# Norms, gates and rotary computed between the pieces of their projections, and a compressed attention branch placed last

## The reference, cut to what matters

```python
# block 1: sparse attention with three branches, gated and summed
o = gb[..., 0:1] * o_cmp + gb[..., 1:2] * o_sel + gb[..., 2:3] * o_win

# block 2: forgetting attention (16 heads of 64)
q, k, v, fz = jnp.split(h @ w_in, [hd, 2 * hd, 3 * hd], axis=-1)
q = rms_norm(q.reshape(B, S, H, 64), q_g)        # k the same way with k_g
log_f = jax.nn.log_sigmoid(fz + fgate_b)
c = jnp.cumsum(log_f, axis=1)                    # added to the logits: c[query] - c[key]

# block 3: one projection, then attention beside a spatial gating
q, k, v, gu, gv = jnp.split(y @ w_in, 5 parts of 512)
q, k = rope(q), rope(k)
gmlp_out = gelu(gu) * (tril(w_s) @ layernorm(gelu(gv)) + b_s)
merged = concat([rmsnorm(attn_out, g_attn), rmsnorm(gmlp_out, g_gmlp)])
```

## Time and profile before

| | |
|---|---|
| median of three runs | 4069.65 us (4064.81 to 4070.16) |
| the profiled execution | 4067.28 us, span on the core 4065.5 us |
| PE / PEld busy | 92% / 84% of the span |
| DVE / ACT / POOL busy | 73% / 45% / 9% |
| granted TensorE clock, mean | 0.953 of full speed |
| DMA | 748.70 MB, mean 184 GB/s |

### The profile page before, as it was taken

How to read it: one execution, slowest core, us unless ns; L and a number is a source line. 1 busy time by engine, 2 the same in 40 slices (tenths; PEclk the granted TensorE clock), 3 DMA queues, 4 the chain that set the end, 5 groups by cost and what they waited for, 6 DMA issues and landing times. The chain is left out here.

```text
span 4065.5 us, 72114 instructions
## 1 busy us (share of the span) xinstructions
PE 3757.7 (92%) x29143; PEld 3408.6 (84%) x29143; DVE 2986.4 (73%) x5894; ACT 1814.9 (45%) x3679; POOL 346.3 (9%) x259
## 2 busy tenths in 40 slices
PE   6999899997899769999999997998999999998698
PEld 6987799996799659989998885898999988897597
DVE  7876778785787677987677856589776787787665
ACT  3444445442454444434444454443444444544343
POOL 0000000000000004830000000086100000000000
PEclk9999899998799879999999997999999999999799
DMA  8766476764166414434444443343444444675253
GB/s 322 277 233 251 172 263 240 264 257 167 57 254 254 155 42 177 153 129 168 172 170 167 158 175 114 114 169 134 146 167 172 171 156 177 244 300 211 94 180 142
DMA packets 119358, 748.70 MB, mean 184 GB/s; under 512 B 13681, under 2 KB 13841, under 8 KB 43761
## 3 DMA queue, kind: packets, MB, share of 16 engines
q1 hardware_dynamic: 117506, 739.92, 49.6%
q10 hardware_dynamic: 688, 3.11, 0.2%
q0 software_dynamic: 832, 1.06, 0.1%
HBM read 741.93 MB, written 1.05 MB: 183 GB/s over the span
## 5 line engine op out<-in xcount | busy, mean ns | idle before, releaser
L930 ACT ACTIVATE weights_high<-weight_ring 128x512 fp32r<-128x512 f32 x2248 | 1294.6, 624 | 1225.6 <-PE bank L196 909.2
L938 DVE TENSOR_TENSOR weights_low<-weight_ring,weights_high 128x512 fp32r<-128x512 f32 x2016 | 1297.1, 686 | 613.4 <-ACT weights_high L930 607.8
L196 PE MATMUL bank<-h_high,weights_high 128*128 128x256 f32 x4800 | 1370.7, 286 | 31.7 <-DVE h_low L682 10.3
L196 PE MATMUL bank<-h_low,weights_high 128*128 128x256 f32 x4800 | 1362.7, 284 | 0.0
L196 PE MATMUL bank<-h_high,weights_low 128*128 128x256 f32 x4800 | 1362.3, 284 | 0.0
L196 PEld LDWEIGHTS bank<-h_high,weights_high 128*128 128x128 f32 x4800 | 924.8, 193 | 51.3 <-issue 27.4
L196 PEld LDWEIGHTS bank<-h_low,weights_high 128*128 128x128 f32 x4800 | 925.4, 193 | 8.7 <-issue 0.2
L196 PEld LDWEIGHTS bank<-h_high,weights_low 128*128 128x128 f32 x4800 | 924.9, 193 | 0.0
L196 PE MATMUL acc<-weights_high,hidden_high 128*128 128x512 f32 x1552 | 613.3, 395 | 0.0
L196 PE MATMUL acc<-weights_low,hidden_high 128*128 128x512 f32 x1552 | 606.4, 391 | 0.0
L196 PE MATMUL acc<-weights_high,hidden_low 128*128 128x512 f32 x1552 | 604.2, 389 | 0.0
(11 more groups left out here) (297 smaller groups left out, 3460.3 us busy)
## 6 DMA issues: line engine op xcount, KB each, us to landing
weight_ring<-stream SPq DMA_DIRECT2D x580, 1024.0 KB, 4.8
h_tok<-slots SPq DMA_DIRECT2D x100, 512.0 KB, 5.8
h_feat<-slots SPq DMA_DIRECT2D x90, 512.0 KB, 5.8
work<-slots SPq DMA_DIRECT2D x26, 512.0 KB, 8.4
mod_sums<-biases SPq DMA_DIRECT2D x7, 1536.0 KB
h_feat<-rows SPq DMA_DIRECT2D x8, 512.0 KB, 4.1
work<-biases SPq DMA_DIRECT2D x1, 1536.0 KB
x_tok<-x ACTq DMA_DIRECT2D x1, 1024.0 KB, 5.4
```

Source lines behind the costliest of these rows:

```text
L196: ins = self.nc.tensor.matmul(out, lhs, rhs, start=start, stop=stop)
L930: act.activation(k.w_hi[:, b, q * self.QUARTER:(q + 1) * self.QUARTER], self.raw(g, q), ACT.Copy).then_inc(k.highs_ready, 1)
L938: return eng.tensor_tensor(k.w_lo[:, b, w], self.raw(g, q), k.w_hi[:, b, w].bitcast(F32), ALU.subtract)
```

## The change

`fox`: `ToTokens`, `ToTokensNarrow`, `HeadNorm` and `ForgetGates` become one stage `ToNormedHeads` (24 halves). `third_mix`: `ToTokens`, both `Keep`, `Rope`, `Spatial` and the second `HeadRms` become one stage `ToTokensAndGate` (20 halves, blocks now in the order gv, gu, q, k, v). Small weights, gains and biases no longer take slots of the stream (five slots fewer) but come by DMAs of their own (`DirectRows`), issued by SP before slot `s + 3` of the stage. Modulation pieces of block 3 move: 14 instead of 8 in the second `carry` of `third_ffn`, 4 instead of 10 in the projection. `nsa`: the causal branches come first, then `Compress` and the compressed branch, which adds; the four row copies move from `ToTokensAndCouples` to the first causal `Scores`, and their destination is `h_feat`.

```diff
+class DirectRows:
+    def __init__(self, k, places, host, before):
+        self.landed = 16 * k.n_direct
+        k.mod_feed[before].append(self)
+    def issue(self, sp, biases, slots, rows):
+        self.host.wait_begun(sp)
+        for i, place in enumerate(self.places):
+            sp.dma_start(place, rows[self.first + i][:, 0:n]).then_inc(self.k.direct_landed, 16)
...
+class ToNormedHeads(ToTokens):
+        self.direct = DirectRows(k, [gates.kept, gains[:, 0:D], gains[:, D:]], self, self.s + 3)
+    def products(self, pe, g, hi, lo):
+        super().products(pe, g, hi, lo)
+        if 4 <= g < 8:
+            self.gates.logits(pe, g - 4)
+        if g == 16:
+            self.gates.add_up(pe)
+    def scalar_after(self, act, g):
+        self.gates.scalar(act, g)
+        if g == 4 * self.N:
+            take_root(k, act, self.stat)
...
+        elif g % 4 == 3:
+            for t in range(TT):
+                act.activation(self.squares[:, t, b * 512:(b + 1) * 512], k.bank[:, (TT * b + t) % NB, :],
+                               ACT.Square).then_inc(k.scalar_for_vector.sem, k.scalar_for_vector.send())
+    def vector_after(self, dve, g):
...
+            for t in range(TT):
+                dve.tensor_tensor(self.qk[:, t, a], k.bank[:, (TT * b + t) % NB, :], self.gains[:, a],
+                                  ALU.mult).then_inc(k.vector_for_tensor.sem, k.vector_for_tensor.send())
+        if g % 4 == 0 and 0 < b <= self.N:
+            ins = dve.tensor_reduce(stat, squares, AX, ALU.add)
...
+        if g == 4 * self.N + 1:
+            dve.reciprocal(self.stat, self.stat).then_inc(k.dve_step, 1)
...
+        piece = g - 4 * self.N - 2
+        if 0 <= piece < 4:
+            dve.tensor_tensor(heads, heads, self.stat[:, at:at + n // 2].unsqueeze(2).to_broadcast(...), ALU.mult)
...
+    def scalar(self, act, g):          # ForgetGates: Abs at 9, Exp at 10, Ln at 12,
+        if g in (13, 14, 17, 18):      # fills of constant rows between them
...
+class ToTokensAndGate(ToTokens):
+        self.direct = DirectRows(k, [norms[:, 0:D], norms[:, D:], self.w..., self.b], self, self.s + 3)
+    def products(self, pe, g, hi, lo):
+        super().products(pe, g, hi, lo)
+        if g == 10:
+            pe.wait_ge(k.vector_for_tensor.sem, k.vector_for_tensor.take())
+            pe.wait_ge(k.vector_for_tensor.sem, k.vector_for_tensor.take())
+            for t in range(TT):
+                for h in range(ROPE_HEADS):
+                    mm = k.mm(k.acc[:, t, a], self.w[:, h, :], self.gv[:, t, a], start=True, stop=True, last=True)
+            mm.then_inc(k.banks_for_vector.sem, k.banks_for_vector.send())
+    def scalar_after(self, act, g):
+        if g == 5:
+            take_root(self.k, act, self.rstd)
+        if g == 14:
+            take_root(self.k, act, self.stat)
+        super().scalar_after(act, g)
+    def vector_after(self, dve, g):
+        super().vector_after(dve, g)
+        if g == 3:
+            self.keep(dve)
+        if 4 <= g <= 8:
+            self.norm(dve, g - 4)
+        if g == 10:
+            dve.wait_ge(k.banks_for_vector.sem, k.banks_for_vector.take())
+            self.gate(dve, 0)
+        if g == 12:
+            self.gate(dve, 1)
+        if 13 <= g <= 16:
+            self.root_mean_square(dve, g - 13)
+        if g == 17:
+            self.rope(dve, 0)
+        if g == 18:
+            self.rope(dve, 1)
...
-    projected = ToTokensAndCouples(k, [(v, None)], feat[:, DC:DC + 4, :], couples)
+    projected = ToTokens(k, [(v, None)])
...
+        if branch == 1:
+            att[0].copy_couples(feat[:, DC:DC + 4, :], couples)
...
-        layers.carry(k.sums[8], 8, (0, 1, 2, 3), 50, 66)
+        layers.carry(k.sums[8], 14, (0, 1, 2, 3), 50, 66)
...
-    projected.carry(k.sums[8], 10, (0, 1, 2, 3), 0, 20)
-    keep = [Keep(k, extra), Keep(k, norms)]
+    projected = ToTokensAndGate(k, gv, gu, qk, v, extra, norms, k.h_tok[:, :, 512:], own, tmp)
+    projected.carry(k.sums[8], 4, (2, 3), 0, 4)
...
-    return [head, projected] + keep + [Rope(k, qk, tmp), ToFeatures(k, qk, qk_t, DC)] + att + [
-            Spatial(k, gu, gv, ...),
+    return [head, projected, ToFeatures(k, qk, qk_t, DC)] + att + [
             HeadRms(k, halves[0], halves[0], 512, norms[:, 1024:1536], None, squares),
-            HeadRms(k, halves[1], halves[1], 512, norms[:, 1536:], None, squares),
```

More of the change, by code:

```diff
@@ L1283, in products @@
                 pe.wait_ge(read.sem, read.take())
+                self.taken[b - NB // TT, t] = read.seen
             self.need(pe, piece)
@@ new lines, in fill @@
+    def fill(self, act, dst, value):
+        n, rows = dst.shape[0], dst.rearrange("p c (t q) -> p (c t) q", q=P)
+        first = HD if n == 1 and value == HD else 0
+        src = self.k.c("ident")[first:first + n].unsqueeze(1).to_broadcast([n, rows.shape[1], P])
+        if value is None:
+            return act.activation(rows, src, ACT.Copy, scale=0.0)
+        one = self.k.small[first:first + 1, ONES:ONES + 1]
+        return act.activation(rows, src, ACT.Identity, scale=0.0, bias=one)
+    def scalar(self, act, g):
+        k, half = self.k, DC // 2
+        if g == 9:
+            act.wait_ge(k.vector_for_scalar.sem, k.vector_for_scalar.take())
+            act.activation(self.tmp, self.z, ACT.Abs).then_inc(k.act_step, 1)
+            self.absolute = k.step("act")
+        if g == 10:
+            act.wait_ge(k.act_step, self.absolute)
+            act.activation(self.tmp, self.tmp, ACT.Exp, scale=-1.0).then_inc(k.act_step, 1)
+            self.exponential = k.step("act")
+        if g == 12:
+            act.wait_ge(k.act_step, self.exponential)
+            act.activation(self.tmp, self.tmp, ACT.Ln, bias=1.0).then_inc(
+                k.scalar_for_vector.sem, k.scalar_for_vector.send())
+        if g in (13, 14, 17, 18):
+            i = (13, 14, 17, 18).index(g)
+            self.fill(act, self.odd[i // 2][0:HD, i % 2 * half:(i % 2 + 1) * half, :], None).then_inc(k.act_step, 1)
+            self.zeroed = k.step("act")
+        if g in (20, 21):
+            a = slice((g - 20) * half, (g - 19) * half)
+            act.wait_ge(k.act_step, self.zeroed)
+            self.fill(act, self.odd[0][0:1, a, :], 0)
+        if g in (10, 16):
+            a = slice(0, half) if g == 10 else slice(half, DC)
+            self.fill(act, self.even[HD:HD + 1, a, :], HD)
@@ L3089, in third_mix @@
     if I is not None:
+        w = I["w_in_3"][0]
+        parts = [w[:, a:a + 512] for a in (2048, 1536, 0, 512, 1024)]
         return [
-            by_columns(I["w_in_3"][0]),
-            params(I["gmlp_w_s_3"][0].transpose(2, 0, 1).reshape(P, -1), I["gmlp_b_s_3"][0].T),
-            rows(I["gmlp_ln_g_3"][0], I["gmlp_ln_b_3"][0], I["g_attn_out_3"][0], I["g_gmlp_out_3"][0]),
+            by_columns(np.concatenate(parts, axis=1)),
             by_rows(I["w_out_3"][0])]
```

392 lines of the change are left out of this document (239 added, 153 removed).

## The result

The changed kernel takes **4025.6 us** (median of 3: 4015.1, 4025.6, 4025.7) against 4069.65: ratio 0.9887, 95% interval 0.986 to 0.9913. In two later groups of runs, each beside the kernel before on the same chip, its ratio was 0.9875 (0.9848 to 0.9901) and 0.9867 (0.9848 to 0.9885). Over all groups the changed kernel has a median of 4015.1 in 11 executions (4013.7 to 4026.7), the kernel before one of 4069.4 in 56 (4062.5 to 4088.9): 54 us. The profiled execution is 4015.1, with a span of 4012.9, against 4067.28: 52.2 us, where the sum had 59.4.

The account below looks back on a forecast made before the run. PE, busy 92%, bounds the dense stages; elsewhere it waits for DVE. 28.5 + 6.9 + 17.7 - 1.2 + 8.0 - 0.5 = 59.4 us off 4067.28 gives 4007.9; forecast 4009, half way to the runs' median, range about 3998 to 4031.

Parts of the forecast that it names:

- its own case: Whole kernel: the forecast itself holds, 4001 to 4014 us, chance 0.68.
- the slack rival: Projections of `third_mix`, `fox`, `third_ffn`: DVE or ACT runs late and PE waits, 18 us less gain, 4027; chance 0.12.
- Part 1: `fox`, projection end to first transpose: 34.15 us shrink to 5.6, gain 28.5 us.
- Part 2: `third_mix`, wait before the transposes: 11.1 us shrink to 4.2, gain 6.9 us (bounds 4 and 9).
- Part 3: `third_mix`, gating moved into the projection and second `HeadRms` gone: gain 17.7 us.
- Part 4: Start of the `third_mix` projection: third modulation piece lands late behind direct rows, cost 1.2 us (bounds 0 and 5).
- Part 5: `nsa`, small projection: second piece lands earlier without the row copies, gain 8.0 us (bounds 0 and 8.5).
- the first rival: `nsa`: the second piece lands late even without the copies, gain only 0 to 2 us, 4017; chance 0.14.
- Part 6: `third_ffn`, last 16 halves: six more modulation pieces, cost 0.5 us (bounds 0 and 4).
- table: Projections: each ACT table switch costs its 1.28 us twice, two on the path, 4012; chance 0.02.
- clock: Both projections: inserted waits keep PE's clock low, halves take 5.4 instead of 2.7 us, up to 4128; chance 0.02.
- the two-halves slack: Dense projections: low parts are made two halves ahead, so DVE may be about 3.4 us late before PE waits.

Follow-up runs that it names:

- b4: Changed kernel with two idle sums (2.4 us) more on DVE at each of four sums in the `fox` projection; `fox` to `ToHeads` 77.4 us against 76.8.
- b3: a4 plus POOL's eight even-head row copies of `fox` issued inside the projection; 4011.2 us, ratio 0.9855.
- c3: c2 with the gating chain of `third_mix` one index earlier; 4006.5 us, ratio 0.9839.
- a2: Changed kernel with the direct rows of `third_mix` issued one stream slot later; 4014.1 us, ratio 0.9861.
- a4: Changed kernel with both four buffers for the `third_mix` pieces and the direct rows one slot later; 4016.0 us, ratio 0.9868.
- c1: Changed kernel with the four row copies issued once more beside the small `nsa` projection, into unread room; projection start to gates' products 21.5 us.
- a3: Changed kernel with four buffers instead of two for the pieces of `third_mix`; 4020.5 us, ratio 0.9886.
- b2: Changed kernel with `nsa` alone put back: compressed branch first, row copies in the small projection; 4021.1 us.
- a1: Changed kernel once more, no edit; 4017.2 us, ratio 0.9875.
- c2: Changed kernel with b3's early `fox` copies and no modulation piece at the start of `third_mix`, all 18 moved to `third_ffn`; 4010.5 us, ratio 0.9857.

## Why the prediction was right, and where not

The forecast was 4009, in the profiled pair the sum gave 4007.9; that execution was 4015.1. The median of the first three executions, 4025.6, is 16.6 above the forecast and outside the 4001 to 4014 that it gave its own case. It lies within the range because that reaches up to 4031, for the slack rival with its 4027. Of that rival only the 5 us for the start of `third_mix` came about, not the waits for DVE and ACT inside the projections. So much was luck: about 10 us of it is which executions came first (the eleven have a median of 4015.1), and the rest is the miss taken apart below. At the other end the range doesn't follow from its terms: the good ends that the parts name, with 1.6 us for the transposes, come to about 4003, not 3998.

By parts, of the one profiled pair and from the timelines above (before's transposes at 2512.89 and 3763.56):

| part | forecast | measured |
|---|---|---|
| 1 `fox` | 28.5 | 29.6 |
| 2 front of `third_mix` | 6.9 | 8.4 |
| 3 gating | 17.7 | 18.6 |
| 4 its start | -1.2 | **-6.8** |
| 5 `nsa`, small projection | 8.0 | 7.7 |
| 6 `third_ffn` | -0.5 | -1.2 to 0 |

**Part 1, right.** The norms and the chain of log-sigmoid are hidden, and DVE and ACT cost nothing: PE waits for no low part in that projection of the changed kernel, and b4 has room to spare. The logits and the sum came to 3.8 and 1.6 us, near the full-clock values of 3.4 and 1.5. The gain is 106.35 - 76.80. That the prediction named the log-sigmoid chain for all of the 24.1 us was a misreading of rows 2, without effect on the sum, as the part was priced by the whole 34.15 us. What was named as next in line, POOL's 16 copies, is so: PE waits 4.99 us for them and a quicker transpose gains nothing, and b3 took 2.6 us out of it.

**Part 2, a little small.** 11.11 - 2.75 = 8.4: DVE ended 2.65 us behind PE (3731.96 against 3729.31), not 4.0, as its last low part was through 5.7 us ahead of PE's end, where the forecast had it due some 4.4 ahead. c3 shows that this tail is what PE waits for.

**Part 3, right.** The stretch from the transposes to `Features` fell by 54.85 - 32.61 = 22.2 us; the gating products put 3.6 back (half 10 takes 6.21 us and half 11 2.86, with 5.44 for two plain ones), 18.6 are left. Over the two traces of before and the three of the changed kernel the 22.2 is anything from 20.7 to 23.1.

**Part 4 is the step that failed.** The forecast had the issue of the third piece right: 3697.6 there is 3664.07 in the time of the changed kernel (PE's first half begins 33.53 us earlier), and it was 3664.39. But it was to land 7.4 us later and came after 9.3. And the low part that came late was priced as its wait alone. Measured, 26.42 - 19.65 = 6.8 us: the wait is 3.55, not 1.1, and behind it halves 3 and 4 take 5.29 and 3.11 us instead of 2.72 each, 3.0 more, as the clock had fallen (0.50 in the window above); the first wait is 0.2 longer. The upper bound of 5 left this second price out too. a2 and a4 show the cause: 1.5 MB of rows ahead of a piece that is needed at once. The forecast had counted these rows, but let the piece land too early behind them. The six traces with this start lose 5.0 to 7.3 us by their first five halves, so 6.8 is near the bad end of the scatter, and every one of them is far from 1.2. Against the forecast this part is 5.6 us worse, in a total that is 6.8 worse by the spans (59.4 forecast, 52.6 measured). Parts 1 to 3 came out 3.5 us better and 4.9 were lost elsewhere (below), so the total is nearer than its terms.

**Part 5, right in the place that it spoke of.** 21.40 - 13.67 = 7.7 us, the wait 0.74 (0.6 forecast), and c1 shows the copies as the cause, so the first rival falls. But the stage as a whole gained 5.1 us in the profiled pair, since the compressed branch's `Values` took 14.45 us instead of 11.39 (4.8 as a mean of all traces, in which the first causal `Values` vary too). The additions that they have to make now are not the reason: DVE's groups of eight instructions take 1.63 us there, as they do without adding, in a3 the same stage takes 11.47, and in b2, where it doesn't add, 14.47. It is the clock, which no part of the sum priced: 0.50 from 1082 us on in the changed kernel, and 1.00 up to 1084 in a3.

**Part 6.** PE has no gap in the window above at a DMA share of 0.99 and 384 GB/s; I had about 370. The stretch takes 198.2 us in a2 and 199.4 in a1 with the same instructions in it, and 198.2 and 199.1 before. The Trainium skill (Perfetto Trace Analysis, section Roofline) gives 358 GB/s as a core's share and says that one core alone can pull more, up to the 435 of its DMA engines; 384 agrees.

**Rivals.** Slack, table and clock (at the lower level through both projections) don't show. The clock is low only behind the two waits at the start. Past that, between half 5 and half 19 of `third_mix` every half but those at the gating takes 2.71 to 2.73 us. A table load of 1.28 us is followed by the next instruction 0.02 us behind it, as in this timeline of ACT of the changed kernel.

```profile
3678.38 1.28 ACT L1347 ACT_TABLE_LOAD   x1
3679.68 0.60 ACT L1347 ACTIVATE work<-bank 128x512 f32<-128x512 f32 x1
```

The measured parts sum to 29.6 + 8.4 + 18.6 - 6.8 + 7.7 = 57.5 us, and the spans differ by 52.6. The other 4.9 lie elsewhere, all but the 1.2 of `third_ffn` (0.5 forecast in part 6) where no part has a price: 1.7 us lost ahead of `nsa`, 2.6 in the rest of `nsa` (3.1 in the compressed `Values`, 0.5 gained elsewhere), 1.2 in `third_ffn`, 0.9 behind `third_mix`, against 0.6 and 1.1 gained in the attention of `fox` and the `peer` behind it, and less in others. Each of these moves by about as much between traces whose code is the same there; what makes them fall out one way or the other is left open.

## What to carry to other kernels

When rows or other bulk are to be fetched beside a stage, place their issue by what stands behind them in the same queue, and by what other queues deliver at that moment, not only by when they are needed themselves. Price a late operand as the wait plus the time at low clock behind it, here another 1.6 to 3.0 us for second waits of 2.7 to 4.5 in seven traces (3.0 for one of 3.55, 1.7 for one of 3.59). And small chains that DVE and ACT make for PE can move into a dense projection as long as each lies within the two-halves slack; an idle load added on purpose, as in b4, is a cheap way to measure it.

## What the runs showed of the hardware

- **The clock in stretches of small products is a matter of the execution.** The first causal `Values` of `nsa` (96 products of 64 columns) take 10.93 us of PE at a granted clock of 1.00, and 18.29 at 0.57, in the same kernel. Timelines of PE of the changed kernel and of a1:

```profile
982.41 10.93 PE L198 MATMUL bank<-work 128*128 128x64 f32 x96 [0.72 <-ACTq L220]
```

```profile
981.10 18.29 PE L198 MATMUL bank<-work 128*128 128x64 f32 x96 [0.72 <-ACTq L220]
```

Windows of the same two, columns as in rows 6:

```profile
982.40:995.10 12.70, 10.93 (x96) 10.79 (x96) 6.50 (x32) 0.00 (x0) 0.00 (x0) 1.00 0.00 0
```

```profile
981.10:1001.10 20.00, 18.29 (x96) 18.10 (x96) 6.51 (x32) 0.00 (x0) 0.00 (x0) 0.57 0.00 0
```

  It was low in four of eleven traces with the new order (a1, a2, a4, b3); the `Values` of `fox` were low in b4, c2 and c3. PE had run the same products ahead of them each time, but not at the same clock: 0.67 from 960 to 970 us in a1, 0.50 from 956 to 979 in the changed kernel. What decides it is left open, and so is whether the new order makes the low case more likely (none of three traces with the old order has it). A single trace can so tell 7 us too much or too little of such a stage.
- **1 MB of POOL's copies** between on-chip buffers delays a 512 KB piece of SP's queue by 5.5 us (11.8 against 6.3), and what the DMA engines move falls from 404 to 243 GB/s at a share of 1.0 and more.
- **POOL issues a copy of one row in 0.48 us** (eight in 3.89), so that sixteen of them behind a barrier are 7.7 us.
